# A hybrid encoder step: fills that run on into the next product, tanh a group ahead, the merge split block by block, and two of three branch products in split passes

## What is computed

```python
cols = einsum('btd,dc->btc', rms_norm(x), w_in)       # mixers A, B, C and three gate blocks
h_a = mlstm(ca);  h_b = sliding_window_attention(cb);  h_c = rwkv7(cc)     # 512 columns each
gates = sigmoid(cg)                                     # 3 x 1024
merged = gates[0]*(h_a @ w_branch_a) + gates[1]*(h_b @ w_branch_b) + gates[2]*(h_c @ w_branch_c)
x = x + rms_norm(merged @ w_out)
gate, up = split(rms_norm(x) @ w_ffn_in)
x = x + rms_norm((silu(gate) * up) @ w_ffn_out)
```

## Time and profile before

| | us |
|---|---|
| median of 3 runs (2477.38 to 2481.17) | 2480.55 |
| the profiled execution | 2479.58 |
| its span, first to last instruction | 2477.8 |
| TensorE matmuls busy | 2354.7 (95%) |
| VectorE busy | 954.7 (39%) |
| ScalarE busy | 867.7 (35%) |
| GpSimd busy | 723.2 (29%) |

### The profile page before, as it was taken

How to read it: one execution, slowest core, us unless ns; L and a number is a source line. 1 busy time by engine, 2 the same in 40 slices (tenths; PEclk the granted TensorE clock), 3 DMA queues, 4 the chain that set the end, 5 groups by cost and what they waited for, 6 DMA issues and landing times.

```text
span 2477.8 us, 52892 instructions
## 1 busy us (share of the span) xinstructions
PE 2354.7 (95%) x23194; PEld 2218.4 (90%) x23194; DVE 954.7 (39%) x1537; ACT 867.7 (35%) x1671; POOL 723.2 (29%) x566
## 2 busy tenths in 40 slices
PE   7999999998999899999989999999999989999997
PEld 7998888888888899999989988888887889999997
DVE  4426645534323432220073275454443325223102
ACT  4344532221343533222344454222324244323222
POOL 3332211111123244444324222111102133444441
PEclk9999999999899999999999999999999999999998
DMA  5532111111214233233334221111112142223331
GB/s 162 142 79 73 52 27 40 40 28 40 59 45 138 60 91 89 86 90 86 82 106 129 61 73 35 41 40 28 40 40 72 52 140 60 86 86 91 86 92 52
DMA packets 334190, 180.78 MB, mean 73 GB/s; under 512 B 33528, under 2 KB 330648, under 8 KB 332936
## 3 DMA queue, kind: packets, MB, share of 16 engines
q1 hardware_dynamic: 333776, 177.34, 25.6%
q10 hardware_dynamic: 184, 0.05, 0.0%
HBM read 167.98 MB, written 9.38 MB: 72 GB/s over the span
## 4 chain that ended last, share of the span: by engine, by line
PE 82%; DVE 9%; ACT 4%; issue 2%; DMA 1%; SPq 0%; POOL 0%; ACTq 0%; DVEq 0%
PE psum_products L636 73%; PE psum_mixer L636 8%; DMA w_raw<-in_w_in 1%; ACT w_high L1189 1%; ACT L1189 1%; DVE x L1619 1%; DVE squares_ffn L1613 0%; DVE c_in_rate L1699 0%; DVE squares L1586 0%; PE psum_mixer L1004 0%; DVE c_kprime L1779 0%; DVE c_kappa_r L1697 0%; DVE c_in_rate L1752 0%; ACT c_kprime L1189 0%; DVE c_kappa_r L1698 0%
## 5 line engine op out<-in xcount | busy, mean ns | idle before, releaser
L2202 POOL TENSOR_TENSOR w_low<-w_raw,w_high 128x512 fp32r<-128x512 f32 (+1 forms) x542 | 697.9, 1309 | 1617.8 <-ACT w_high L1189 1617.3
L636 PE MATMUL psum_products<-xn_high,w_high 128*128 128x272 f32 (+1 forms) x3424 | 738.0, 297 | 27.4 <-DVE xn_low L1568 12.3
L636 PE MATMUL psum_products<-xn_high,w_low 128*128 128x272 f32 (+1 forms) x3424 | 711.8, 289 | 0.0
L636 PE MATMUL psum_products<-xn_low,w_high 128*128 128x272 f32 (+1 forms) x3424 | 709.1, 289 | 0.0
L636 PEld LDWEIGHTS psum_products<-xn_high,w_high 128*128 128x128 f32 x3424 | 544.1, 190 | 48.3 <-issue 20.1
L636 PEld LDWEIGHTS psum_products<-xn_low,w_high 128*128 128x128 f32 x3424 | 543.5, 190 | 0.0
L636 PEld LDWEIGHTS psum_products<-xn_high,w_low 128*128 128x128 f32 x3424 | 540.1, 190 | 0.0
L1189 ACT ACTIVATE w_high<-w_raw 128x512 fp32r<-128x512 f32 (+1 forms) x542 | 308.0, 617 | 215.2 <-PE psum_products L636 134.1
L636 PE MATMUL psum_products<-hidden_high,w_high 128*128 128x272 f32 x704 | 145.9, 288 | 0.0
L636 PE MATMUL psum_products<-hidden_high,w_low 128*128 128x272 f32 x704 | 145.7, 288 | 0.0
L636 PE MATMUL psum_products<-hidden_low,w_high 128*128 128x272 f32 x704 | 145.1, 288 | 0.0
(11 more groups left out here) (361 smaller groups left out, 2877.3 us busy)
## 6 DMA issues: line engine op xcount, KB each, us to landing
w_raw<-in_w_in SPq DMA_DIRECT2D x112, 512.0 KB, 4.0
w_raw<-in_w_ffn_in SPq DMA_DIRECT2D x88, 512.0 KB, 3.8
w_raw<-in_w_ffn_out SPq DMA_DIRECT2D x32, 512.0 KB, 3.8
w_raw<-in_w_out SPq DMA_DIRECT2D x16, 512.0 KB, 4.0
w_raw<-in_w_ffn_out SPq DMA_DIRECT2D x16, 384.0 KB, 3.3
x_kept<-x SPq DMA_DIRECT2D x2, 2176.0 KB, 7.5
x<-x_kept SPq DMA_DIRECT2D x2, 2176.0 KB, 9.7
w_raw<-in_w_in SPq DMA_DIRECT2D x16, 256.0 KB, 3.7
```

Of the source, the lines that this page charges most:

```text
L636: return pe.matmul(out, lhsT, rhs, start=start, stop=stop, skip_group_check=True)
L2202: low_ready.inc(pool.tensor_tensor(wl[:, n % NSPLIT, ks_], wraw[:, slot, ks_], wh[:, n % NSPLIT, ks_].bitcast(F32), ALU.subtract))
```

## The change

- The first and third branch products become split products (`unsplit` leaves only the second plain). Their inputs get a high part (ScalarE, `a_out_high`, `c_finish`) and a low part (VectorE, `a_out_low`, `c_out_low`). For the first branch this is a new item `a_out_split`, ahead of the first gate product.
- `fill` goes on into the product after the next one; it never takes products of the third branch. `c_chain` gets `fill(1)` between the solve and its users and `fill(3)` at the end.
- The tanh of group g + 1 is done at level 3 of group g (`tanh_ahead`); group 0 keeps its own in `c_prep`.
- Each block of `merged` but the last is split right after the following third-branch product.

```diff
-        plan += [("gate", l) + GATES[0], ("c_shift_out", l)]
+        plan += [("a_out_split", l), ("gate", l) + GATES[0], ("c_shift_out", l)]
...
-UNSPLIT = {"branch"}
+def unsplit(s):
+    return s[0] == "branch" and s[2] == 1
...
             def product(s, steps=8):
...
-                    rhs = [(acols[:, AQ + k, :], bh[:, k, :], cc[:, k, :])[b] for k in range(4)]
-                    gemm(s, rhs=rhs, nk=4, steps=steps)
+                    if b == 0:
+                        gemm(s, rh=a_high, rl=a_low, nk=4, steps=steps)
+                    elif b == 1:
+                        gemm(s, rhs=[bh[:, k, :] for k in range(4)], nk=4, steps=steps)
+                    else:
+                        gemm(s, rh=c_high, rl=c_low, nk=4, steps=steps)
...
+            def fillable(s):
+                return (s[0] in ("cols_b", "cols_c", "gate") or (s[0] == "cols_a" and 12 <= s[2] < 16)
+                        or (s[0] == "branch" and s[2] < 2 and s[3] > 0))
...
+                u = unit_at[0]
+                while steps > 0 and u < len(units) and u < unit_at[0] + 2 and fillable(units[u]):
+                    s = units[u]
+                    there = done_k.get(s, 0)
+                    product(s, steps)
+                    steps -= done_k[s] - there
+                    u += 1
...
                 bank[1].filled(last, "dve")
+                fill(1)
                 bank[1].claim(pe)
...
-                fill(4)
+                fill(3)
...
+            def tanh_ahead(l, g):
+                n, at, nch, L = c_group(g)
+                step(fn(tanh_w[:, 0:n], cc[0:64, 12, at:at + n], ACT.Tanh), flow("c_tanh_w"))
...
-                step(fn(tanh_w[:, 0:n], cc[0:64, 12, at:at + n], ACT.Tanh), flow("c_tanh_w"))
+                    tanh_ahead(l, 0)
...
+            def c_finish(l, f):
+                flow("c_out").wait_next(act, "act")
+                step(fn(c_high[:, f, 0:T], cc[:, f, 0:T], ACT.Copy), flow("c_out_high"))
+
+            def a_out_high(l):
+                flow("a_out").wait_next(act, "act")
+                for h in range(4):
+                    step(fn(a_high[:, h], acols[:, AQ + h, :], ACT.Copy), flow("a_out_high"))
...
+            def merge_high(k):
+                flow("merged").wait_next(act, "act")
+                xh_ready.inc(fn(xh[:, k, :], merged[:, k, :], ACT.Copy, scale=0.5))
+
             def merge_split(l):
...
+                merge_high(KD - 1)
...
+                elif kind == "branch" and s[2] == 2 and s[3] > 0:
+                    merge_high(s[3] - 1)
+                elif kind == "c_level":
+                    if s[3] == 3 and s[2] + 1 < GROUPS:
+                        tanh_ahead(s[1], s[2] + 1)
...
+                if f:
+                    c_out_low(f - 1)
                 if f == 3:
...
+                    c_out_low(3)
...
+            def a_out_low(l):
+                for h in range(4):
+                    flow("a_out_high").wait_next(dve, "dve")
+                    step(tt(a_low[:, h, :], acols[:, AQ + h, :], a_high[:, h].bitcast(F32), SUB), flow("a_h") if h == 3 else None)
...
+                if b == 2 and m:
+                    merge_low(l, m - 1)
```

More of the change, by code:

```diff
@@ L458, in build, with __getitem__ @@
     y_tok = place("y_tokens", [P, 5, D], arena)
+    a_low = place("a_out_low", [P, 4, T], acols_at + 4 * AQ * T, F32R)
+    a_high_at = ((a_rb_at + 4 * (2 * 1024 + 2 * 512) + 31) // 32 * 32, (rest + 4 * 4 * T + 31) // 32 * 32)
+    assert a_high_at[0] + 4 * 2 * T <= bh_at and a_high_at[1] + 4 * 2 * T <= acols_at + 4 * AQ * T
+    a_high_two = [place(f"a_out_high{i}", [P, 2, T], at_, F32R) for i, at_ in enumerate(a_high_at)]
+    class Blocks:
+        def __getitem__(self, key):
+            return a_high_two[key[1] // 2][key[0], key[1] % 2]
+    a_high = Blocks()
     ctx = ExitStack()
@@ L502, in build @@
         unit_no = {s: i for i, s in enumerate(units)}
-        split_units = [s for s in units if s[0] not in UNSPLIT]
+        split_units = [s for s in units if not unsplit(s)]
         split_no = {s: i for i, s in enumerate(split_units)}
@@ L702, in product @@
                          wait_k=s in steps_of, steps=steps)
+            def fillable(s):
+                return (s[0] in ("cols_b", "cols_c", "gate") or (s[0] == "cols_a" and 12 <= s[2] < 16)
+                        or (s[0] == "branch" and s[2] < 2 and s[3] > 0))
             def fill(steps):
-                if unit_at[0] < len(units):
-                    s = units[unit_at[0]]
-                    if (s[0] in ("cols_b", "cols_c", "gate") or (s[0] == "cols_a" and 12 <= s[2] < 16)
-                            or (s[0] == "branch" and s[3] > 0)):
-                        product(s, steps)
+                u = unit_at[0]
[5 more added lines that the diff above has]
+                    u += 1
             steps_of = set()
@@ L1977, in branch, with merge_low @@
                     step(tt(merged[:, m, :], merged[:, m, :], dst, ADD), flow("merged") if b == 2 else None)
+                if b == 2 and m:
+                    merge_low(l, m - 1)
+            def merge_low(l, k):
+                dve.wait_ge(xh_ready.sem, split_base(l, 2) + k + 1)
+                step(stt(out=xl[:, k, :], in0=merged[:, k, :], scalar=0.5, in1=xh[:, k, :].bitcast(F32),
+                         op0=MUL, op1=SUB), xl_ready)
             def hidden_low(j):
@@ L2004, in _ @@
                 elif kind == "merge_split":
-                    for k in range(KD):
-                        dve.wait_ge(xh_ready.sem, split_base(l, 2) + k + 1)
-                        step(stt(out=xl[:, k, :], in0=merged[:, k, :], scalar=0.5, in1=xh[:, k, :].bitcast(F32),
-                                 op0=MUL, op1=SUB), xl_ready)
+                    merge_low(l, KD - 1)
                 elif kind == "ffn_gate":
```

22 lines of the change are left out of this document (12 added, 10 removed).

## The result

The changed kernel takes **2465.39 us** (median, 2462.70 to 2466.26) against 2480.01 for the kernel before on the same chip: ratio 0.995, 95% interval 0.9937 to 0.9963 (the two medians alone give 0.994, inside it). It is faster, by 12 us by the ratio and 15 by these medians, where 40 were forecast, and lies above the range (2423 to 2458).

The account below looks back on a forecast made before the run. TensorE, busy 95% of the span, was taken as the bound. Gains of 27.3 us a layer less losses of 7.1 gave 20.2, times two 40.4, so 2439.7 us; forecast 2431 to 2448, wider range 2423 to 2458.

Parts of the forecast that it names:

- Third branch: Its 8 products a layer, as split products, take 3.01 us instead of 3.67: gain 5.3 us a layer.
- rival 4: Split branch products: three passes are no cheaper than the plain product, 20 us lost, 2460; chance 0.05.
- rival 3: Third branch: VectorE becomes the bound, 4.26 us a product instead of 3.01, 2459; chance 0.10.
- Merge: Between last branch product and first output product: splitting block by block gains 5.7 us a layer.
- Tanh ahead: Delta-rule groups: tanh one group ahead removes its waits except group 0's; gain 4.1 us a layer.
- negated solution: Chain: its 9 waits a layer, 5.8 us, each get one filling step; gain 4.0 us a layer.
- Fills that run on: Delta-rule stage: filled waits vanish for 0.2 us per interruption; gains 4.0, 1.6, 0.6 and 1.4 us a layer.
- group 2: Delta-rule stage: a 1.66 us wait on low weights goes, 0.3 left for the next; gain 1.4 us.
- Group 0: First token group: first-branch copies and subtractions delay its keys; first preparation matmul 1.8 us later, a loss.
- First branch: Its eight products become 0.66 us cheaper, seven counted since the first lies in group 0; gain 4.6 us a layer.
- rival 2: New waits of groups 0, 1 and 3 each bring a 3.4 us half-clock stretch, costing 1.7; 2449; chance 0.12.
- rival 5: GpSimd's queue: late low parts make TensorE stand 11.0 us in all five groups; slower, 2535; chance 0.02.

Follow-up runs that it names:

- tanh_chain: Changed kernel with the first branch plain and fills stopping at the current product's end; 0.9842 of the kernel before, 2441 us.
- gpsimd_more: tanh_chain plus seven pairs a layer of GpSimd subtractions of constants, where a split first branch's low weights would be made; 0.9888 of the kernel before, 2452 us.
- short_branch: tanh_chain with the fourth k-step of each first-branch product left out, so TensorE alone does less; 0.9809 of the kernel before, 2433 us.
- keys_deep: Changed kernel with fills running on into the next product only in c_keys and c_scale; 0.9859 of the kernel before, 2445 us.
- deep_late: Changed kernel, run-on only in c_keys, c_scale and c_gram, four first-branch subtractions behind group 0's first key product; 0.9843 of the kernel before, 2441 us.

## Why the prediction was wrong

- **Third branch, 5.3 a layer**: right. 3.01 us a product on TensorE, so rival 4 falls. VectorE fits for six products and falls behind at the last two, which costs no more than the 0.82 us ahead of the output product; rival 3 falls in size.
- **Merge, 5.7**: 4.9 came (7.3 us for 12.2). Both parts alone measured 21 of 22.
- **Tanh ahead (4.1) and negated solution (4.0)**: right in size, in tanh_chain even a little low. The waits named went. But the second of them was booked under fills that run on, and tanh_chain shows that it hardly needs run-on: 14 of the 18 waits are gone with the fill in the chain alone.
- **The step that failed is "Fills that run on"**: it priced each filled wait by the wait, less 0.2 us for the interruption, and took the filling work for free. It is not. Products taken at waits of 0.3 to 1 us are missing at the keys, the one place where the data's latency leaves TensorE several microseconds. With run-on confined to the keys, 23 us come back (0.9950 to 0.9859), TensorE's waits on low weights fall from 19.2 to 7.7 us and those on gate_tanh from 11.7 to none. What was lost there the forecast sought in the weights alone (groups 1 and 3, 3.56 and 3.53 measured for 3.5 and 3.7). It had no term for the PSUM pair: group 2 was booked as +1.4 and got waits of 0.94 and 2.72; group 4 was booked at 1.8 and waits 3.15 on gate_tanh and 1.13 on c_scratch. Nor had it one for the products of mixer C's finish, which were pulled ahead into group 4: that stage waits 1.9 us more.
- **Group 0, +1.8**: the delay of the key chain (5.9 us) was right, its price was not. It was read at the next matmul, and the 3.44 us where the cover ends were left out, 2.3 of them from GpSimd's low parts beside VectorE's keys.
- **First branch, 7 x 0.66**, 9.2 us in both layers: its worth depends on the fills. The split is 20 us worse than plain without run-on, equal within the intervals with run-on at the keys (2445 and 2443), and some 6 us better with run-on everywhere. The term counted TensorE's time only. gpsimd_more and short_branch show two costs beside it, each in part: the weights' low parts queue ahead of others that are waited for, and shorter products cover less.
- **The sum.** Two times the 10.8 us missing in delta rule and finish, plus 2 x 0.8 at the start and 2 x 1.2 in branch and merge, is 25.6, and 2439.7 + 25.6 = 2465.3. The four new waits without a term (3.44 in group 0, 3.4 beyond the plan in group 2, 2.5 in group 4, 1.9 in the finish) add up to 11.2, about those 10.8. In the stages of layer 0, TensorE's idle time was to fall by 6.4 us and rose by 3.6, which is 10.0 of the 10.8. Layer 1 was not added up wait by wait; doubling takes it as equal.
- **Half clock (rival 2)**, given 0.12, came in part. The changed kernel, behind the waits of groups 0, 1 and 3 in layer 0; then the kernel before, behind the tanh wait of group 1 and at the end of group 4:

```profile
345.00:355.00 10.00, 6.56 (x77) 5.44 (x76) 4.46 (x4) 2.17 (x5) 4.42 (x4) 0.83 0.01 2
415.00:430.00 15.00, 11.44 (x73) 11.22 (x72) 10.71 (x10) 6.79 (x11) 8.36 (x5) 0.77 0.06 19
560.00:570.00 10.00, 6.47 (x40) 6.24 (x39) 2.84 (x5) 9.77 (x13) 4.20 (x4) 0.83 0.10 28
```
```profile
400.00:410.00 10.00, 10.00 (x70) 7.35 (x69) 4.85 (x7) 5.26 (x12) 2.12 (x2) 0.83 0.01 2
655.00:675.00 20.00, 17.81 (x209) 14.45 (x208) 6.56 (x16) 3.84 (x8) 4.94 (x4) 0.66 0.29 75
```

  With 1.2 and 2.4 GHz as the two levels, that is 3.4, 6.9 and 3.4 us at the lower one against 3.4 and 13.6: new stretches behind the new waits, as the rival said, and a long one gone. The delta stage's mean of 0.97 in both kernels hides this. Waits are the larger part: between the changed kernel and keys_deep, 14.1 us are idle time and 7.1 busy time of the same instructions.
- **GpSimd's queue (rival 5)** is real in kind, 3.5 us in two groups, and far from 11 in five.

## What to carry to other kernels

Filler work is a stock, not a gift. Give it to the longest latency first, and before a fill may reach further ask what the next long wait will be covered with. A product pulled ahead needs its weights, its result buffer and that buffer's reader ahead as well, and all three are in other engines' queues in the old order. Price a delay where its cover ends, not at the first instruction that is late.

## What the hardware showed

The same group 4 of the same kernel (deep_late), layer 0 and layer 1, with idle times of 4.81 and 4.82 us:

```profile
605.39:667.45 62.06, 57.25 (x677) 49.97 (x675) 26.36 (x71) 20.60 (x42) 12.40 (x12) 0.83 0.20 50
1809.65:1864.90 55.25, 50.43 (x679) 44.94 (x676) 26.37 (x71) 20.61 (x42) 12.41 (x12) 0.97 0.22 54
```

The same work with the same idle time, 6.8 us apart, at a mean granted clock of 0.83 and 0.97 of 2.4 GHz. The kernel before shows the same kind of difference between its layers (0.88 from 616 to 675 us, 0.97 from 1838.3 to 1894). Differences of 5 us between two profiles are therefore not read as a mechanism here without the clock beside them, and medians of several runs decide.

VectorE's key products beside GpSimd's low parts took 1.64, 1.63 and 1.09 us; the same three took 0.69 each in the kernel before, with GpSimd idle. GpSimd's four low parts took 1.38 each, where two of that shape took 1.25 each with VectorE idle (2.50 us at 343.15 in the kernel before). The Trainium skill, SBUF — State Buffer, "Who interferes with whom", has a VectorE instruction with two SBUF inputs contend with a GpSimd instruction that reads SBUF, for a port pair that it calls an exclusive lock. The rows agree that the two slow each other. VectorE pays the more, up to 0.95 us, and the sum of both, 0.69 + 1.25 = 1.94, was not reached.
